# A decoder layer on one core: the input projection's first weights, its first scale, its last sweep and the first heads' q and k

## What is computed

```python
mod = (silu(c) @ w_ada + b_ada)                    # shift, scale, gate, twice
h = rms_norm(x, norm1_w) * (1 + sc1) + sh1
proj = h @ w_in          # q | k | v | z | xBC | dt | gate_attn | gate_ssm
# branch A: stick-breaking attention, 8 heads x 64, sample tokens read cached pages of k and v
# branch B: causal conv, SSD scan, grouped norm
x = x + g1 * merged(branch A, branch B) @ w_out
h = rms_norm(x, norm2_w) * (1 + sc2) + sh2
x = x + g2 * peer(h)     # 16384 single-neuron experts, 8 heads, top 16
```

## Time and profile before

| | |
|---|---|
| median of 3 executions | 4578.85 us (4577.56 to 4583.16) |
| the profiled execution | 4576.29 us, of which its span is 4574.6 us |
| PE busy | 4258.6 us, 93% of the span |
| DVE busy | 3172.3 us, 69% |
| ACT busy | 1417.4 us, 31% |
| POOL busy | 983.2 us, 21% |
| mean granted TensorE clock | 0.956 of 2.4 GHz |

### The profile page before, as it was taken

How to read it: one execution, slowest core, us unless ns; L and a number is a source line. 1 busy time by engine, 2 the same in 40 slices (tenths; PEclk the granted TensorE clock), 3 DMA queues, 4 the chain that set the end, 5 groups by cost and what they waited for, 6 DMA issues and landing times. The chain is left out here.

```text
span 4574.6 us, 67889 instructions
## 1 busy us (share of the span) xinstructions
PE 4258.6 (93%) x24256; PEld 2504.0 (55%) x24256; DVE 3172.3 (69%) x5611; ACT 1417.4 (31%) x1943; POOL 983.2 (21%) x1020
## 2 busy tenths in 40 slices
PE   5999995899988899979899999999978999999997
PEld 2665663344456466656555556556644555555554
DVE  5347324555568533465788989888968898988985
ACT  3333420333321112232224444444432222222221
POOL 0000001433300001100033222222233333333330
PEclk8999997899999799989999999999989999999998
DMA  5753756555334577734477777777689888888881
GB/s 210 243 197 104 232 191 181 172 167 159 118 112 156 217 243 245 287 105 147 148 264 277 269 276 256 280 266 282 253 299 342 290 304 292 293 299 288 305 280 40
DMA packets 422558, 1039.46 MB, mean 227 GB/s; under 512 B 38498, under 2 KB 209122, under 8 KB 413730
## 3 DMA queue, kind: packets, MB, share of 16 engines
q0 software_dynamic: 112896, 396.43, 26.9%
q1 hardware_dynamic: 251970, 403.51, 25.6%
q10 hardware_dynamic: 57440, 236.35, 13.6%
HBM read 809.88 MB, written 226.27 MB: 226 GB/s over the span
## 5 line engine op out<-in xcount | busy, mean ns | idle before, releaser
L443 PE MATMUL totals_ps<-act_parts,v_parts 128*128 128x416 f16 x6144 | 1082.9, 339 | 42.7 <-DVE act_parts L3202 42.4
L443 PE MATMUL dot_ps<-h_parts,u_parts 128*128 128x416 f16 x6144 | 1114.9, 340 | 6.8 <-issue 6.8
L443 PEld LDWEIGHTS totals_ps<-act_parts,v_parts 128*128 128x128 f16 x6144 | 601.5, 98 | 522.9 <-issue 44.6
L443 PEld LDWEIGHTS dot_ps<-h_parts,u_parts 128*128 128x128 f16 x6144 | 594.4, 98 | 460.1 <-issue 11.6
L456 PE MATMUL in_ps<-h_parts_in,in_parts 128*128 128x384 f16 (+1 forms) x3168 | 514.5, 319 | 4.5 <-DVE in_parts L808 4.5
L3277 POOL DMA_INDIRECT rows_in<-in_v,row_v x204 | 301.5, 1478 | 499.1 <-DVE h L3221 486.2
L456 PEld LDWEIGHTS in_ps<-h_parts_in,in_parts 128*128 128x128 f16 x3168 | 310.5, 98 | 170.6 <-DVE in_parts L808 4.6
L2555 POOL DMA_INDIRECT u_rows_in<-tmp_u_rows,row_u x192 | 251.1, 1308 | 577.3 <-DVE row_dot L2897 548.8
L3141 ACT ACTIVATE v_parts<-v_group,units 128x1024 f16<-128x1024 f32 x128 | 136.9, 1138 | 766.5 <-PE totals_ps L443 738.1
L2657 ACT ACTIVATE gelu<-dot_ps,units 128x416 f32<-128x416 f32 x256 | 155.4, 607 | 629.2 <-PE dot_ps L443 592.6
L3213 DVE SCALAR_TENSOR_TENSOR h<-totals_ps,sum_unit,h 128x416 f32<-128x416 f32 x388 | 248.3, 648 | 139.7 <-PE totals_ps L443 139.2
(11 more groups left out here) (395 smaller groups left out, 5925.2 us busy)
## 6 DMA issues: line engine op xcount, KB each, us to landing
u_chunks<-in_u SPq DMA_DIRECT2D x128, 512.0 KB
v_group<-in_v SPq DMA_DIRECT2D x31, 2048.0 KB
tmp_g<-gelu ACTq DMA_DIRECT2D x128, 416.0 KB
tmp_w<-h ACTq DMA_DIRECT2D x26, 2048.0 KB
w_groups<-tmp_w SPq DMA_DIRECT2D x32, 1664.0 KB
gelu_in<-tmp_g SPq DMA_DIRECT2D x31, 1664.0 KB
tmp_u_rows<-proj_rows ACTq DMA_DIRECT2D x64, 512.0 KB, 5.4
attend_v_sweep<-in_v ACTq DMA_DIRECT2D x64, 512.0 KB, 4.3
```

The lines of the kernel that those rows point to most:

```text
L443: mm = pe.matmul(bank, left(x), right(y), start=first and x == 0 and y == 0, stop=last and x == 1)
```

## The change

- `in_ring` and its semaphores are made before ada_phase, and SP issues the four loads of the first weights at the end of ada_phase's list, behind the ada weights. To make room, the squares of the first norm go into h's buffer, which is written with h only later.
- The scale of h no longer comes from a reduction over h. `modulated` forms a bound beside the gain: twice the larger of the largest gain times 32 (with a little room) and the largest shift. These are two reductions over 72 elements a partition and three small instructions. project_phase copies the bound instead of reducing h. The bound is larger than the true maximum, so h gets a smaller power of two.
- v's sweep at the end of project_phase has four buffers instead of two.
- q and k of heads 0 and 1 have their buffers from project_phase on. SP loads them there, behind the last ring load, once the chunks 0 to 7 are stored, and waits for them before it waits for v. attend_phase only raises their semaphores.

```diff
-            h_top=keep("h_top", [P, 1]),
+            h_top=keep("h_top", [P, 2]),
...
+            with nc.sbuf_tensor("q", [HD, 2, SEQ], F32) as s["q"], nc.sbuf_tensor("k", [HD, 2, SEQ], F32) as s["k"], \
+                    nc.sbuf_tensor("v_tok", [P, TILES + 1, AW], F32) as s["v_tok"]:
+                with nc.sbuf_tensor("in_ring", [P, RING, KC, P], F32) as s["w_in"]:
+                    s["w_in_loaded"] = [sem(f"w_in{u}") for u in range(RING)]
+                    with nc.sbuf_tensor("x", [P, KC, T], F32) as s["x"]:
+                        ada_phase(nc, a, s, sem)
+                    project_phase(nc, a, s, sem)
...
-def modulated(dve, link, s, src, dst, norm_w, shift, scale, scaled):
+def modulated(dve, link, s, src, dst, norm_w, shift, scale, scaled, bound=None):
...
+    if bound is not None:
+        link.mark(dve.tensor_reduce(bound[:, 0:1], gain[:, :, :].rearrange("p k q -> p (k q)"), AX.X, ALU.max,
+                                    apply_absolute_value=True))
+        link.link(dve.tensor_reduce(bound[:, 1:2], sh.rearrange("p k q -> p (k q)"), AX.X, ALU.max,
+                                    apply_absolute_value=True))
+        link.link(dve.tensor_scalar(bound[:, 0:1], bound[:, 0:1], D ** 0.5 * (1 + 2.0 ** -10), None, ALU.mult))
+        link.link(dve.tensor_tensor(bound[:, 0:1], bound[:, 0:1], bound[:, 1:2], ALU.max))
+        link.mark(dve.tensor_scalar(bound[:, 0:1], bound[:, 0:1], 2.0, None, ALU.mult))
...
-        norm = Norm(nc, sem, "norm1", s["x"], s["y"], s, sum_ps)
+        norm = Norm(nc, sem, "norm1", s["x"], s["h"], s, sum_ps)
...
                 load_ada(range(GROUPS // 2, GROUPS))
+                for u in range(RING):
+                    sp.dma_start(s["w_in"][:, u, :, :], a["w_in"][u]).then_inc(s["w_in_loaded"][u], 16)
...
-        v_sweep = Sweep(nc, ctx, sem, "proj_v", s["v_tops"], 2, sweep.buf[1:3])
+        v_sweep = Sweep(nc, ctx, sem, "proj_v", s["v_tops"], 4, sweep.buf)
...
-                for u in range(RING):
-                    sp.dma_start(ring[:, u, :, :], a["w_in"][u]).then_inc(w_in[u], 16)
                 sp.dma_start(state[:, :, :, :], a["state_conv"]).then_inc(wide_in, 16)
...
+                for u in range(2):
+                    sp.wait_ge(stored[u], 16 * (1 + CH_Z // 2))
+                for u in range(2):
+                    rows = slice(u * HD, (u + 1) * HD)
+                    sp.dma_start(s["q"][:, u, :], a["proj"][0, rows, 0:SEQ]).then_inc(heads_in, 16)
+                    sp.dma_start(s["k"][:, u, :], a["k_out"][0, rows, 0:SEQ]).then_inc(heads_in, 16)
+                sp.wait_ge(heads_in, 64)
                 sp.wait_ge(v_taken, 1 + TILES + 1)
...
-                largest(S_H, h[:, :, :].rearrange("p k t -> p (k t)"))
+                link.mark(dve.tensor_copy(scales.tops[:, S_H:S_H + 1], s["h_top"][:, 0:1]))
                 found(0)
...
-                load(0, 0)
-                load(1, 1)
+                for u in range(2):
+                    sp.sem_inc(qk_in[u], 32)
                 sp.dma_start(pages[:, :], a["pages"]).then_inc(pages_in, 16)
```

More of the change, by code:

```diff
@@ L267, in vector @@
         dve.wait_ge(self.scaled, NS)
-def modulated(dve, link, s, src, dst, norm_w, shift, scale, scaled):
+def modulated(dve, link, s, src, dst, norm_w, shift, scale, scaled, bound=None):
     gain = s["gain"]
-    link(dve.tensor_scalar(gain[:, :, :], s["mod"][:, scale:scale + KC, :], 1.0, None, ALU.add))
+    link.link(dve.tensor_scalar(gain[:, :, :], s["mod"][:, scale:scale + KC, :], 1.0, None, ALU.add))
     w = s["par"][:, norm_w:norm_w + KC].unsqueeze(2).to_broadcast([P, KC, 1 + NSEQ])
-    link(dve.tensor_tensor(gain[:, :, :], gain[:, :, :], w, ALU.mult))
+    link.link(dve.tensor_tensor(gain[:, :, :], gain[:, :, :], w, ALU.mult))
     sh = s["mod"][:, shift:shift + KC, :]
+    if bound is not None:
[6 more added lines that the diff above has]
+        link.mark(dve.tensor_scalar(bound[:, 0:1], bound[:, 0:1], 2.0, None, ALU.mult))
     def per_seq(t):
@@ L285, in modulated @@
     own = dst[:, :, SEQ:T].rearrange("p k (s l) -> p k s l", l=LS)
-    link(dve.tensor_tensor(own, own, per_seq(gain), ALU.mult))
+    link.link(dve.tensor_tensor(own, own, per_seq(gain), ALU.mult))
     dve.tensor_tensor(own, own, per_seq(sh), ALU.add)
@@ L537, in copy_rows @@
                                     mod_ps[:, g, :]).then_inc(rows_ready, 1)
-                link = Chain(dve, chain).link
+                link = Chain(dve, chain)
                 for g in range(GROUPS // 2):
@@ L546, in _ @@
                 offset = s["par"][:, W_BADA:W_BADA + MOD_FIRST].unsqueeze(2).to_broadcast([P, MOD_FIRST, N])
-                link(dve.tensor_tensor(s["mod"][:, 0:MOD_FIRST, :], turn_ps[:, :, :], offset, ALU.add))
-                modulated(dve, link, s, s["x"], s["h"], W_N1, 0, KC, h_scaled)
+                link.link(dve.tensor_tensor(s["mod"][:, 0:MOD_FIRST, :], turn_ps[:, :, :], offset, ALU.add))
+                modulated(dve, link, s, s["x"], s["h"], W_N1, 0, KC, h_scaled, s["h_top"])
 def project_phase(nc, a, s, sem):
@@ L559, in sb @@
             return ctx.enter_context(nc.sbuf_tensor(name, shape, F32))
-        ring = sb("in_ring", [P, RING, KC, P])
+        ring, w_in = s["w_in"], s["w_in_loaded"]
         w16 = ctx.enter_context(nc.sbuf_tensor("in_parts", [P, 2, RING, KC, P], F16))
@@ L578, in project_phase @@
         ps_dt = ctx.enter_context(nc.psum_tensor("dt_ps", [P, 512], F32))
-        w_in = [sem(f"w_in{u}") for u in range(RING)]
         wide_in = sem("wide_in")
@@ L590, in project_phase @@
         dt_summed, dt_taken = sem("dt_summed"), sem("dt_taken")
-        rows_out = sem("rows_out")
+        rows_out, heads_in = sem("rows_out"), sem("first_heads_in")
         h = s["h"]
```

5 lines of the change are left out of this document (2 added, 3 removed).

## The result

The changed kernel takes **4534.85 us** (median of 4 runs, 4527.69 to 4537.59). The kernel before took 4578.2 beside it (4577.46 to 4583.16). The ratio, as it was estimated with its interval, is 0.989, 0.9873 to 0.9906; 0.9914 was forecast, just outside. It is faster, and by more than I said. But against the 4578.2 beside it the ratio is worth 50 us (0.011 x 4578.2; 43 to 58 by the interval), where 39.4 was forecast, the bounds of my sum ended at 43.1 and the range allowed 47.9 (4578.85 - 4531). The two medians alone lie 43.4 us apart, and the two profiled executions 38.7.

The account below looks back on a forecast made before the run. PE, busy 93% of the span, was taken as the bound, so gains had to come from stretches where it had nothing to do: 8.2 + 26.7 + 4.5 = 39.4 us off 4578.85 gives 4539.4, range 4531 to 4553.

Parts of the forecast that it names:

- part 2: End of project_phase: with four sweep buffers loads are hidden and attend_phase starts 26.7 us earlier (24.7 to 29.3).
- meeting and clearing: Between project_phase's block end and attend_phase: semaphore work taken to cost 4.4 us more, as before.
- Part 1: Start of project_phase: early ring loads and the bound save 9.3 us, new instructions cost 1.1; net 8.2 (7.8 to 8.6).
- SP's leg: End of project_phase: last v copy to SP's last write landing takes 13.6 us (11.0 to 15.6).
- Part 3: Start of attend_phase: early q and k bring the first page load and PE's scores forward, gaining 4.5 us (2.5 to 5.2).
- the shift reaches the end: After the three gains: later stages begin when the one before ends, so the whole 39.4 us stays.
- the price of the page table: Start of attend_phase: landing within SP's 2.34 us of issue gains 5.2 us; 5.04 us as before gains 2.5.
- A: End of project_phase: sweep loads get no faster with more in flight; gain 12.7 us, time 4566; chance 0.11, full or partial.
- B: attend_phase: gives nothing, PE's 10.32 us page wait stays; gain 34.9 us, time 4544; chance 0.10.
- C: End of project_phase: v's writes are short, DVE's end decides; up to 7.2 us more, time 4532; chance 0.09.
- D: Whole kernel: slower, as 79 us more PE work at the low clock eats the gain; chance 0.02.
- E: ada_phase: ring loads mix with the ada weights and delay their second half; under 1 us; no chance of its own.

Follow-up runs that it names:

- start_alone: The changed kernel with two buffers in v's sweep and q and k of heads 0 and 1 loaded in attend_phase again; 4571.55 us, ratio 0.998.
- changed_again: The changed kernel once more, unedited, against the kernel before; 4530.81 us, ratio 0.9891.
- sweep4_alone: The kernel before with only v's sweep changed, from two buffers to four; 4543.81 us, ratio 0.9917.

## What the prediction had right, and the step that failed

The three places were right, the size was not. The step that failed is a term of the sum, part 2's 26.7 us, which measured 33.0. It took the 4.4 us behind DVE's last sweep for a fixed price of meeting and clearing, where 3.2 of them were POOL's drain, and it took SP's writes at 13.6 us, where they took 9.9.

**Part 1** was right in its place, and nearly in its size. Forecast 9.3 in the project stage; 8.0 measured alone, with both halves needed, as said. The first split did come 9.3 us sooner against the stage's start (8.8 us behind it instead of 18.1, in start_alone and in all three profiles of the changed kernel). Most of what is missing at the stage's end is the clock again. In start_alone and in two of the three profiles of the changed kernel PE fell once more to the lower level soon after it had begun, for 3.4 us; in changed_again and in the kernel before it did not. Three microseconds of that, first in the changed kernel's first profile, then in changed_again:

```profile
94.50:97.50 3.00, 3.00 (x12) 1.53 (x11) 2.68 (x4) 0.00 (x0) 0.00 (x0) 0.50 0.42 175
```
```profile
94.50:97.50 3.00, 3.00 (x22) 2.07 (x21) 2.67 (x4) 0.38 (x1) 0.00 (x0) 1.00 0.42 175
```

Half of 3.4 is 1.7. From the stage's start to the first v tile changed_again is 10.0 us shorter than the kernel before, the other three 7.5 to 8.0, and its project stage is the shortest of the changed kernel's, 667.1 against 670.2 and 669.5. The ada stage grew by 0.6 us by the means of the stages (less than the 1.2 by which the two profiles of before differ), forecast 1.1 (0.7 to 1.5): the five instructions with their links span 58.58 to 59.51, 0.93 us. A reduction of 72 elements took 0.23, against the 0.25 chosen.

**Part 2** was right in its place: sweep loads hidden (6.2 us each, where 6.4 was said to be the limit), tiles 8.65 apart, DVE ahead of SP, SP last. The step that failed is the last of its sum, "the meeting and clearing of semaphores cost 4.4 us more", together with the 13.6 us taken for SP's writes. Alone (sweep4_alone) it gave 33.0 us, forecast 26.7 (24.7 to 29.3), outside my own bounds. Two terms make the difference. I read 4.42 us between DVE's last sweep and the next stage as a fixed cost. 3.2 of it was POOL's drain behind its last sweep load, which the change takes out of the way. And SP's leg took 9.9 us, below the 11.0 that I had called the lower bound. There I had subtracted the time of two loads and kept the pace of the rest; in fact 0.56 MB, about one load, fell out of the stretch, and all of it ran at 344 GB/s instead of 293. Together 3.2 + 3.7 = 6.9, for 6.3 seen. In the profile after, the same sum closes: attend_phase was forecast at 746.5 and starts at 741.95. The last v copy ends at 730.65 instead of 728.5 (+2.1; the tiles' start moved by 6.1, 8.6 and 7.2 us in the three profiles, 8.2 forecast), SP's leg gives 3.7 and the drain 3.2, which makes 741.7.

**Part 3** was right up to its first use: first scores at the stage's start, SP's first page load 4.0 us after it (745.95 against 741.95; 4 to 5 forecast), and PE's wait for pages ending 40.4 us after the start instead of 45.05, 4.7 sooner (4.5 forecast). What failed here is "the shift reaches the end", which took the rest of the stage as unchanged. Inside the same stage each long step behind a head's start takes 1.7 to 3 us back, the changed kernel had all three in each profile, and by the means some 2 us of the shift are left over all kernels and 0.8 in the changed one. As to the price of the page table, the Trainium skill (DMA: Bandwidth & Descriptors, section Anatomy of one DMA) has a fixed 2.0 us per transfer and then its bytes. That section gives the figure for transfers that POOL issues, and the page table is SP's. By that rule it would land ahead of SP's last issue. The trace after agrees so far as it can show: SP no longer waits for the table (2.7 us in the earlier trace rows), and POOL's first page load, which needs the table, is issued at 744.77, 2.7 us after the table's own issue at 742.05, where with loads of 256 KB ahead of it the table had needed 5.04 us.

**The rivals.** A (loads no faster) is false: no wait for loads is left. B (attention gives nothing) is false in its mechanism, since PE's wait did end sooner, and nearly true in its number. C (v's writes are short) is half true: 9.9 us, and SP still last. D did not come in the form I gave it: the clock's mean rose from 0.956 to 0.960. But the clock moved single stages: 1.7 us behind the start of the projection, and in attend_phase what ate part 3. E is not seen: the second half of the ada weights was in time for PE, which is busy throughout 40 to 42.

**The time** came out at 4534.85 against 4539.4. In stages, by the means of the profiles: 0.6 lost in ada_phase, 42.2 won in project_phase and 0.8 in attend_phase, and 1.5 lost behind them, 41.0 in all, against 39.4. That this lies so near is luck in part: part 2 gave 6.3 more than forecast, and parts 1 and 3 gave less. The three groups of runs give 50 (interval 43 to 58), 50 and 41 us by their ratios, and 43.4, 50.6 and 37.7 by their medians. What they have beyond 41.0 has no stage of its own, and is of the size by which the kernel before differs from itself.

## What to carry to other kernels

Where all engines meet, look up when each one's drain begins and ends before you call the time behind the last work a fixed cost; an engine that issued DMAs late can hold the meeting, and moving its last issues forward or to another queue takes that away. Two arms that end together must be shortened together, and a transfer's duration read in a crowded stretch is no lower bound once the crowd moves. A gain of a few microseconds at a stage's start should be followed to that stage's end in several profiles, with those of the kernel before repeated too, since here one unchanged stage went from 512.8 to 520.0. Where a stage's length comes in steps, as with the long steps here, compare executions that have the same number of them: that brought out 4.4 to 5.5 us which the means hid.

## What the runs showed of the hardware

POOL's drain at the end of project_phase lasted 8.1 to 11.0 us from its last load (8781, 10668, 8127 and 11045 ns in the rows above), longer than the median load takes to land in either kernel (4.2 us and 6.2); SP's drain behind writes it had waited for took 7 ns, and ACT's behind 8 sweep loads of its own 14 ns. PE's clock stayed at its lower level for 8.5 or for 12.1 of 15 us behind the same gap in two executions of one kernel. With four loads of v in flight instead of two the stretch of the tiles went from 169 to 225 GB/s, and a load from 4.2 to 6.2 us.
